# A two-block transformer on one core: who scales the first layer's softmax rows

## The reference, cut to what matters

```python
s_own = jnp.einsum('hqd,hkd->hqk', qc, k_own).astype(jnp.float32) * ATTN_SCALE
s_own = s_own + bias_ht[:, t5_bucket(jnp.maximum(dist_own, 0))]
s_own = jnp.where((dist_own >= 0)[None], s_own, NEG_INF)
logits = jnp.concatenate([s_sel.reshape(H, Q_CHUNK, n_sel * MOBA_BLOCK), s_own], axis=-1)
p = jax.nn.softmax(logits, axis=-1).astype(v.dtype)
return (jnp.einsum('hqnk,hqnkd->hqd', p_sel, v_sel)
        + jnp.einsum('hqk,hkd->hqd', p_own, v_own))
```

## Time and profile before

| | us |
|---|---|
| median of 3 runs | 1907.91 (1905.82 to 1908.23) |
| the profiled execution, its own time | 1906.45 |
| its span, first to last instruction | 1904.7 |
| PE busy / DVE / ACT / POOL | 1822.7 / 1096.6 / 744.2 / 116.1 |
| PE's share of the chain that ended last | 90% |
| the first layer's attention | about 144 to 191 |

### The profile page before, as it was taken

One profiled execution on the slowest core, in us unless ns is written; L12 is line 12 of the kernel. 1 busy time (PEld: TensorE's weight loads), 2 busy tenths in 40 slices (PEclk: granted clock), 3 DMA queues, 4 the chain that ended last, 5 costly groups with the idle time before them and its releaser, 6 DMA issues.

```text
span 1904.7 us, 23381 instructions
## 1 busy us (share of the span) xinstructions
PE 1822.7 (96%) x8886; PEld 1459.6 (77%) x8886; DVE 1096.6 (58%) x1637; ACT 744.2 (39%) x1057; POOL 116.1 (6%) x116
## 2 busy tenths in 40 slices
PE   5987999999999989989999999999988999999998
PEld 4884688888887777768888888877855788888886
DVE  6988454444333665544676773347997366767422
ACT  4226343333323224443544542222147344445221
POOL 0000010000011100531000000100000100000000
PEclk9998999999999999999999999999989999999999
DMA  4420123223233411112222232332310132222321
GB/s 156 154 93 19 45 89 110 88 91 107 88 111 100 144 67 45 53 37 79 99 98 100 88 110 89 111 122 71 107 45 2 45 111 88 95 103 88 110 89 67
DMA packets 25896, 167.29 MB, mean 88 GB/s; under 512 B 3132, under 2 KB 3260, under 8 KB 6754
## 3 DMA queue, kind: packets, MB, share of 16 engines
q1 hardware_dynamic: 23328, 158.83, 24.1%
q0 software_dynamic: 1920, 6.42, 1.2%
q10 hardware_dynamic: 576, 1.05, 0.2%
HBM read 163.10 MB, written 2.13 MB: 87 GB/s over the span
## 4 chain that ended last, share of the span: by engine, by line
PE 90%; DVE 5%; ACT 3%; issue 2%; DMA 0%; DVEq 0%; SPq 0%; ACTq 0%
PE ps L398 25%; PE ps L400 25%; PE ps L399 25%; PE ps L558 2%; PE ps L539 2%; PE ps L586 2%; ACT ring L945 1%; PE ps L413 1%; PE ps L412 1%; PE ps L411 1%; ACT w_hi L798 1%; DVE w_lo L1139 1%; DVE ring L1370 1%; PE ps L622 1%; PE ps L624 1%
## 5 line engine op out<-in xcount | busy, mean ns | idle before, releaser
L398 PE MATMUL ps<-a_hi,w_hi 128*128 128x512 f32 x1616 | 637.0, 394 | 8.2 <-DVE a_lo L1145 3.8
L400 PE MATMUL ps<-a_hi,w_lo 128*128 128x512 f32 x1616 | 629.9, 390 | 0.0
L399 PE MATMUL ps<-a_lo,w_hi 128*128 128x512 f32 x1616 | 629.7, 390 | 0.0
L398 PEld LDWEIGHTS ps<-a_hi,w_hi 128*128 128x128 f32 x1616 | 303.9, 188 | 84.5 <-issue 17.4
L399 PEld LDWEIGHTS ps<-a_lo,w_hi 128*128 128x128 f32 x1616 | 304.0, 188 | 64.5 <-issue 2.6
L400 PEld LDWEIGHTS ps<-a_hi,w_lo 128*128 128x128 f32 x1616 | 303.8, 188 | 64.0
L1139 DVE TENSOR_TENSOR w_lo<-raw,w_hi 128x2048 fp32r<-128x2048 f32 x82 | 192.3, 2345 | 241.8 <-ACT w_hi L798 241.7
L798 ACT CAST w_hi<-raw 128x2048 fp32r<-128x2048 f32 x82 | 156.0, 1902 | 350.6 <-PE ps L400 299.0
L398 PE MATMUL ps<-h_hi,w_hi 128*128 128x512 f32 x528 | 206.2, 391 | 0.0
L400 PE MATMUL ps<-h_hi,w_lo 128*128 128x512 f32 x528 | 205.4, 389 | 0.0
L399 PE MATMUL ps<-h_lo,w_hi 128*128 128x512 f32 x528 | 205.4, 389 | 0.0
(11 more groups left out here) (226 smaller groups left out, 1930.5 us busy)
## 6 DMA issues: line engine op xcount, KB each, us to landing
raw<-weights_dram SPq DMA_DIRECT2D x148, 1024.0 KB, 4.9
bias_t<-bias_rows_scratch POOLq DMA_DIRECT2D x8, 256.0 KB, 4.5
ncb<-decay_rows_scratch POOLq DMA_DIRECT2D x8, 256.0 KB, 5.1
out_dram<-xT SPq DMA_DIRECT2D x8, 256.0 KB, 2.0
xT<-x_in_dram ACTq DMA_DIRECT2D x4, 256.0 KB, 6.1
xT<-x_in_dram SPq DMA_DIRECT2D x4, 256.0 KB, 8.8
v<-pT POOLq DMA_DIRECT2D x1, 1016.0 KB, 6.6
vec<-vectors_dram SPq DMA_DIRECT2D x1, 282.5 KB, 3.5
```

The source lines that it names most:

```text
L398: pe.matmul(dst, wh, hi[:, k0 + k, :], start=start and k == 0, stop=False)
L399: pe.matmul(dst, wh, lo[:, k0 + k, :], start=False, stop=False)
L400: last = pe.matmul(dst, wl, hi[:, k0 + k, :], start=False, stop=stop and k == nk - 1)
```

## The change

VectorE keeps the reciprocals of the first layer and no longer multiplies; ScalarE gets a new function `scaled`, which waits for the reciprocal and multiplies each lane of the unit in place, by a Copy whose scale is read from `stat`. In ACT's step i it stands between the exponentials of unit i+3 and the move of unit i, and it handles unit i+2, as the removed VectorE instructions did. The other kinds of attention keep their code.

```diff
+            def scaled(u):
+
+                a = (2 * u.n) % 8
+                wait("rc", u.k)
+                for lane in range(2):
+                    e = lane_ring(u, lane)
+                    A.activation(e, e, ACT.Copy, scale=stat[:, a + lane, 2:3]).then_inc(sem["pr"], 1)
+
@@ ACT, attend, one step
                             exps(run[a])
+                    if 0 <= a - 1 < n and run[a - 1].kind == "moba":
+                        scaled(run[a - 1])
@@ DVE, factors
                 Vv.reciprocal(stat[:, a:a + 2, 2:3], stat[:, a:a + 2, 1:2]).then_inc(sem["rc"], 1)
                 wait("rc", u.k)
+                if u.kind == "moba":
+                    return
                 if u.kind != "diff":
```

## The result

| | before | after |
|---|---|---|
| median (lowest to highest) | 1907.20 us (1905.82 to 1908.23), 5 runs | 1917.04 us (1916.91 to 1917.94), 5 runs |
| the profiled execution | 1906.45 | 1917.94 |
| its span | 1904.7 | 1916.1 |

The ratio of the two is 1.0055, 95% interval 1.0043 to 1.0066: the kernel became slower by some 10 us. The prediction said 1915.4 within 1910 to 1919, slower by 7.5. The direction and the mechanism were right, and the size was 2.3 us short: TensorE's lower clock came into two places where the sum had no term for it.

What follows compares the result with a forecast made beforehand. The prediction took the stage to be bound by a ring of handovers with ScalarE on every leg. First group 1.5, two steady groups 4.4 and end 1.6 gave +7.5 us: 1915.4 from a median of 1907.91, range 1910 to 1919.

Steps and rivals of the forecast that it cites:

- The reading of the stage: First layer's attention: a ring of handovers between three engines sets the time, with 10.74 us per group of four units.
- leg: A piece of a group's 10.74 us, from one ACT instruction's start to another's; seven were listed, 0.52 to 4.41 us.
- The price: A pair of ScalarE multiplications costs 1.22, 1.02, 0.80 and 0.59 us at 512, 384, 256 and 128; 3.63 a group.
- The steady group: Groups between the 512-wide L1370 of units 7, 11 and 15: +2.21 us each to 12.95; two give +4.4.
- the 0.62 that came back: 128-wide exponentials follow the copies after 0.30 us, not 0.92, as VectorE has 0.88 less ahead of its 128-wide L1370.
- The first group: Start of the stage: PE's six transposes start at 156.0 in place of 154.49, +1.5 us; PE's chain behind unchanged.
- The end: Behind the last 512-wide exponentials: six transposes at 187.44 in place of 185.82, +1.6 us; PE's work and cast follow.
- The sign of being wrong: Trace after: a group under 11.5 us, or PE's granted clock below 1.00 after the first group, would refute the forecast.
- The lower clock: Rival: longer waits drop PE to its lower clock in one or two groups, +4 to +8 us, 1919 to 1923; 8%.
- The packed ScalarE: Rival: ACT runs without a gap, 11.0 us a group, some +1.5 us in all, 1909.4; 6%.
- the two long legs: Copies 384 to exponentials 512 (4.41 us) and cast to exponentials 256 (1.68 us); both forecast to stay as they were.
- the marks named: Expected in the trace after: groups of 12.9 us, ACT busy 0.88, DVE idle some 3 us a group, last cast near 197.7.

Runs made afterwards that it cites:

- act_padded: VectorE multiplies as in the kernel before, while ScalarE does 32 multiplications of the changed kernel's form, sizes and place into a scratch tile; 1916.32 us, ratio to before 1.0053.
- dve_padded: The changed kernel, with VectorE still doing 32 multiplications of the same sizes into a scratch tile; 1916.62 us, ratio to the kernel before 1.0053.
- taps_moved: The kernel before, with the convolution's tap of every fourth step done one step earlier on VectorE; 1904.61 us, ratio to before 0.9989.
- const_scale: The changed kernel, with a constant as factor of ScalarE's multiplications in place of the reciprocal read from memory; 1914.51 us, ratio to the kernel before 1.0043.
- only_512: Against the kernel before, ScalarE multiplies only the four 512-wide units and VectorE the other twelve; 1911.97 us, ratio to before 1.0031.
- warm_end: The changed kernel, with four more PE products of 256 columns ahead of the transposes of units 13 and 14; 1914.75 us, ratio to the kernel before 1.0042.
- copies_first: The changed kernel, with ScalarE's multiplications behind the copies to pT of the same step; 1914.90 us, ratio to the kernel before 1.0047.
- end_on_dve: The changed kernel, but VectorE multiplies the last two units (14 and 15); 1913.77 us, ratio to the kernel before 1.0036.

## Why the prediction was right, point by point

**The reading of the stage.** VectorE had the largest share and was not the bound; ScalarE had the smallest and stood on every leg. act_padded and dve_padded show it from both sides: holding ScalarE alone costs the whole of the loss, and giving VectorE its work back costs nothing. Cutting the wait of one leg shortens the kernel (taps_moved).

**The price.** 0.61 at 512 was right (a pair 1.23 in the trace), and so was what was worked out for the other widths (1.01, 0.79, 0.58 against 1.02, 0.80, 0.59). const_scale shows that the read of the factor, 0.09, is in it. The comparison with VectorE mixed two measures: from start to start VectorE's 512-wide pair is 0.80 (174.88 to 175.68), so ScalarE needs 1.5 times as long, not 1.4. Nothing in the sum hangs on it.

**The steady group.** +2.21 forecast, +2.19 measured, with each leg within 0.02. One reason in it was wrong, though its number was right: the 0.62 that came back was put down to VectorE having 0.88 us less ahead of the 128-wide L1370. The pair that stands there is the 384-wide one, and the 512-wide one of 0.88 us stands behind (174.88 in the earlier trace rows). The kernel before, DVE:

```profile
172.94 0.75 DVE L1389 TENSOR_SCALAR ring<-ring,stat 128x384 f32<-128x384 f32 x2
173.60 0.75 DVE L1316 SCALAR_TENSOR_TENSOR cacc<-cu,vec,cacc 128x512 f32<-128x512 f32 x1
174.27 0.28 DVE L1370 CUSTOM_DVE_ANT_0 ring<-ps,bias_t 128x128 f32<-128x128 f32 x1
```

And the relief was not needed: in dve_padded the 0.62 comes back without it. ScalarE arrives 1.01 us later by its own multiplications of 384, and the wait is over by then. In only_512 neither happens, since VectorE keeps the 384-wide pair and ScalarE doesn't arrive later: the wait stays (0.51), and the group is 10.74 + 1.22.

**The first group.** +1.5 forecast, +2.6 measured. This is the first of two steps that failed. The prediction said that behind the six transposes "PE's chain is what it was". It was not: the clock was granted at 0.50 from 156 to 160, and the way from these transposes to the 512-wide L1380 took 7.07 us (156.85 to 163.92) in place of 6.28. The kernel after:

```profile
154.06 1.09 PE L558 MATMUL ps<-sq_f,ring 128*128 128x128 f32 x4 [2.96 <-ACT pT L973]
155.07 0.69 PE L586 MATMUL ps<-pT,v 128*64 128x128 f32 x4
...
156.85 1.54 PE L558 MATMUL ps<-sq_f,ring 128*128 128x128 f32 x6
158.32 1.12 PE L586 MATMUL ps<-pT,v 128*64 128x128 f32 x8
159.38 1.51 PE L539 MATMUL ps<-qk 64*128 64x384 f32 x4
```

The last two took 0.94 and 0.92 in the kernel before, and from start to start they hold the whole 0.79. The six transposes came at 156.85, where 156.0 and the 0.54 of the start make 156.5. ScalarE's copies were on time (155.98); PE was late, since its four transposes and the values behind them ran at the low clock (1.09 and 0.69, before 0.63 and 0.49). In other kernels with the same order on ScalarE this group was 12.18 to 13.60, so its size isn't a fixed one; the 12.18 is dve_padded's, where the clock was 0.93 from 158 to 160.

**The end.** +1.6 forecast, +3.07 measured, the second step that failed. ScalarE's part was right to 0.01 (4.47 to the transposes), and "what PE does behind it" does not follow at the old pace: it took 1.44 us more at a clock of 0.50. warm_end takes exactly that away. So the last cast came at 200.81 and not near 197.7: 0.54 by the start, 1.1 by the first group and 1.44 here.

**The sign of being wrong.** The prediction named two, and one of them, PE's granted clock below 1.00 after the first group, came true at the end of the stage (0.50 from 195 to 197). The ring was read rightly, and the full clock that the sum took for granted was not there.

**The rivals.** The lower clock was priced at +4 to +8 for one or two whole groups, and given 8 in 100. It came in a smaller form, in half of the first group and at the end, for some 2.5 us in all (0.8 + 0.3 + 1.4), on top of the forecast. Adding it as a term would have given 1917.9, near the 1917.04 measured. That the time lay inside the forecast's own 1911.5 to 1918 all the same is in part luck: its upper part was there for a dearer multiplication, and the multiplication was not dearer. The packed ScalarE did not come: the two long legs kept their 4.40 and 1.69. Of the marks named, VectorE's idle time was under-read: 5.5 us of 13, not 3.

**Still open.** Why the same wait lowers the clock in one group and not in another (below), and 0.9 us between the profiled executions behind this stage.

## What to carry to other kernels

In a ring of handovers the engine with the smallest busy share can be the one that sets the time: cut one period of the timeline into legs from start to start, and ask of each new instruction whether it stands in a leg's wait or in its work. Work taken off an engine counts only where someone waits for that engine at that place. And where a change makes TensorE wait in longer pieces, put the clock in the sum as a term of its own, for the stretches where it was low before and where the waits grow.

## What the runs showed of the hardware that was not expected

PE's waits of about the same length went with either clock. In the kernel after, both steady groups have among others a wait of 1.61 or 1.60 and one of 0.79 us, and the granted clock stays at 1.00. In dve_padded the wait of 0.80 in the second group is followed by six transposes of 1.51 us where 0.85 is usual, and the wait of 1.61 in the third by eight of 1.89 where 1.06 is usual; in only_512 a wait of 1.40 is followed by 0.85 in one group and by 1.51 in the next. With 2.25 us (copies_first) it fell in both steady groups, but behind 2.31 us at the end of dve_padded four transposes took the usual 0.63. So the length of the last wait doesn't decide it, and what does isn't in these rows.

What a fall costs depends on where it comes. Ahead of the eight transposes it made a group of 12.94 one of 14.52 (dve_padded, end_on_dve). Ahead of the six it cost 0.36 in only_512 (12.32 in place of 11.96), and nothing in the second group of dve_padded and the third of end_on_dve, both 12.94: PE was slower where it would have waited next, and the wait of 1.61 was gone. The second group of dve_padded, with the clock at 0.57 from 168 to 172:

```profile
168.67 1.51 PE L558 MATMUL ps<-sq_f,ring 128*128 128x128 f32 x6 [0.80 <-ACT pT L973]
...
172.56 1.07 PE L558 MATMUL ps<-sq_f,ring 128*128 128x128 f32 x8
```

Four products of 256 columns, some 0.5 us each, in the waits of 1.98 and 0.65 us at the end were enough to hold the clock at 1.00 (warm_end). The Trainium skill, "TensorE: Matmul & The Clock Gate", section "HAM oscillation — how this bites in real kernels", describes a loop in which groups of matmuls stand between waits, for DMA there, and start at the lower clock after each wait. These rows agree that waits between products can bring the clock down, and differ in that shorter waits, for ScalarE, did so here and not each time.
